# Issue order of half-height and half-width float32 products in four places of a transformer kernel

## The reference, cut to what matters

```python
# first block, sliding window attention: 8 heads of 64, 2 kv heads, window blocks of 128
s = jnp.einsum('bnqkgd,bnjkd->bnkgqj', qb, kk) * (HEAD_DIM ** -0.5)
...
o = jnp.einsum('bnkgqj,bnjkd->bnqkgd', p, vv)
# second block, first layer, latent attention: 8 heads, 128 wide without and 64 wide with rotation
s = (jnp.einsum('bqhd,bkhd->bhqk', qn, k_nope)
     + jnp.einsum('bqhr,bkr->bhqk', qr, k_rope)) * scale
# second layer, gated linear recurrence in chunks of 64 tokens, 8 heads of 128
new_state = (jnp.exp(G_last[:, :, 0, :])[..., None] * state
             + jnp.einsum('bhsd,bhse->bhde', kc * jnp.exp(G_last - G), vc))
```

## Time and profile before

| what | value |
|---|---|
| three timed runs | 3094.95, 3084.0, 3091.87 us |
| median | 3091.87 us |
| span of the profiled execution, first to last instruction | 3085.2 us |
| TensorE busy in it | 2936.1 us, 95% |
| mean granted TensorE clock | 0.984 |

### The profile page before, as it was taken

How to read it: one execution, slowest core, us unless ns; L and a number is a source line. 1 busy time by engine, 2 the same in 40 slices (tenths; PEclk the granted TensorE clock), 3 DMA queues, 4 the chain that set the end, 5 groups by cost and what they waited for, 6 DMA issues and landing times. The chain is left out here.

```text
span 3085.2 us, 42539 instructions
## 1 busy us (share of the span) xinstructions
PE 2936.1 (95%) x14433; PEld 2462.7 (80%) x14433; DVE 1818.4 (59%) x2998; ACT 1118.9 (36%) x2318; POOL 1818.0 (59%) x1154
## 2 busy tenths in 40 slices
PE   6989999999999899999999989999999999999998
PEld 5757899999999777778777667888778887788886
DVE  8764168968566488888763453222367887422226
ACT  2232225555565244444443423220135552322103
POOL 5425686676888655555534135666566674466673
PEclk9999999999999999999999999999999999999999
DMA  8422354555799999999952012233221111222331
GB/s 315 151 69 81 100 160 138 188 192 181 266 328 331 361 374 410 404 411 399 404 220 82 28 48 95 95 98 101 88 89 62 62 62 48 82 95 95 102 102 69
DMA packets 168332, 538.97 MB, mean 175 GB/s; under 512 B 16160, under 2 KB 73632, under 8 KB 151712
## 3 DMA queue, kind: packets, MB, share of 16 engines
q1 hardware_dynamic: 82544, 301.62, 28.2%
q0 software_dynamic: 18432, 134.23, 10.8%
q10 hardware_dynamic: 67248, 101.86, 9.2%
HBM read 485.21 MB, written 52.43 MB: 174 GB/s over the span
## 5 line engine op out<-in xcount | busy, mean ns | idle before, releaser
L2539 POOL TENSOR_SCALAR whi<-ring 128x1024 fp32r<-128x1024 f32 x384 | 424.1, 1104 | 969.6 <-issue 477.2
L2541 POOL TENSOR_TENSOR wlo<-ring,whi 128x1024 fp32r<-128x1024 f32 x384 | 969.8, 2526 | 32.1
L562 PE MATMUL ps<-norm_hi,whi 128*128 128x384 f32 (+1 forms) x1288 | 490.5, 381 | 15.9 <-ACT A L1414 8.8
L564 PE MATMUL ps<-norm_hi,wlo 128*128 128x384 f32 (+1 forms) x1288 | 452.4, 351 | 0.0
L563 PE MATMUL ps<-norm_lo,whi 128*128 128x384 f32 (+1 forms) x1288 | 450.4, 350 | 0.0
L562 PE MATMUL ps<-whi,mixed_hi 128*128 128x512 f32 x768 | 304.4, 396 | 25.8 <-DVE wlo L2133 23.5
L2565 POOL TENSOR_TENSOR wlo<-ring,whi 128x512 fp32r<-128x512 f32 x126 | 174.1, 1382 | 231.3 <-ACT whi L1518 231.3
L563 PE MATMUL ps<-wlo,mixed_hi 128*128 128x512 f32 x768 | 302.3, 394 | 0.0
L564 PE MATMUL ps<-whi,mixed_lo 128*128 128x512 f32 x768 | 302.2, 394 | 0.0
L562 PE MATMUL ps<-mix_hi,whi 128*128 128x512 f32 x744 | 290.7, 391 | 0.0
L564 PE MATMUL ps<-mix_hi,wlo 128*128 128x512 f32 x744 | 289.4, 389 | 0.0
(11 more groups left out here) (364 smaller groups left out, 6033.7 us busy)
## 6 DMA issues: line engine op xcount, KB each, us to landing
ring<-stream SPq DMA_DIRECT2D x519, 512.0 KB, 3.5
gelu_map<-A ACTq DMA_DIRECT2D x128, 192.0 KB, 2.9
gate_map<-A ACTq DMA_DIRECT2D x48, 512.0 KB, 5.1
A<-gelu_map ACTq DMA_DIRECT2D x128, 192.0 KB, 11.7
A<-gate_map ACTq DMA_DIRECT2D x31, 768.0 KB, 11.8
A<-ada_w SPq DMA_DIRECT2D x10, 2048.0 KB, 8.0
A<-ada_w SPq DMA_DIRECT2D x4, 1024.0 KB, 22.6
X<-x_in SPq DMA_DIRECT2D x1, 2048.0 KB, 18.6
```

The lines of the kernel that those rows point to most:

```text
L562: first = mm(out_, lh, rh, start=start, stop=False)
L564: return first, mm(out_, ll, rh, start=False, stop=stop)
L2539: g.tensor_scalar(h[:], raw[:], 1.0, 0.0, ALU.mult, ALU.add).then_inc(whi_ready, 1)
L2541: g.tensor_tensor(rest[:], raw[:], h[:].bitcast(F32), ALU.subtract).then_inc(split_ready, 1)
```

## The change

Nothing is computed differently; only the order of issue on TensorE changes. Window scores and values alternate between the halves; the latent attention issues both full products first and then the two half ones; the state changes go in the order of the chunks, so that even and odd ones alternate, and each of the last two raises `delta_ready`.

```diff
@@ win_scores(u)
-                for g in range(4):
+                for g in (0, 2, 1, 3):
                     h = kv * 4 + WIN_ORDER[g]
@@ products with the values
-                for g in range(4):
-                    h = WIN_ORDER[g]
+                for g0 in range(2):
                     for kb in kbs:
                         t0 = (n - 1 + kb) * P
-                        last = mm(ps[64 * (h % 2):64 * (h % 2) + 64, 6, (h // 2) * P:(h // 2) * P + P],
-                                  A[:, PV, t0 + kv * 64:t0 + kv * 64 + 64], ptv[:, g * 2 + kb, :],
-                                  start=kb == kbs[0], stop=kb == 1)
+                        for g in (g0, g0 + 2):
+                            h = WIN_ORDER[g]
+                            last = mm(ps[64 * (h % 2):64 * (h % 2) + 64, 6, (h // 2) * P:(h // 2) * P + P],
+                                      A[:, PV, t0 + kv * 64:t0 + kv * 64 + 64], ptv[:, g * 2 + kb, :],
+                                      start=kb == kbs[0], stop=kb == 1)
@@ mla_scores(m)
                     mm(out_, A[:, QN + h, n * P:(n + 1) * P], A[:, KN + h, 0:(n + 1) * P], start=True, stop=False)
+                for g in range(2):
+                    out_ = ps[:, 2 + g, 0:(n + 1) * P]
                     r = slice(64 * g, 64 * g + 64)
                     last = mm(out_, A[r, QR + pair, n * P:(n + 1) * P], A[r, DOWN + 4, 0:(n + 1) * P], start=False,
                               stop=True)
@@ state changes
-            def hgrn_delta(h, odd):
+            def hgrn_deltas(h):
                 if h:
                     pe.wait_ge(state_ready, (NCH - 1) * h)
-                for c in range(odd, NCH - 1, 2):
+                for c in range(NCH - 1):
+                    odd = c % 2
                     r = slice(64 * odd, 64 * odd + 64)
                     w = slice((c // 2) * P, (c // 2) * P + P)
-                    last = mm(ps[:, 3 + 2 * odd, w], A[r, HKT, w], A[r, HV + h % 2, w], start=True, stop=True)
-                last.then_inc(delta_ready, 1)
+                    ins = mm(ps[:, 3 + 2 * odd, w], A[r, HKT, w], A[r, HV + h % 2, w], start=True, stop=True)
+                    if c >= NCH - 3:
+                        ins.then_inc(delta_ready, 1)
...
-                            hgrn_delta(b, 0)
-                            hgrn_delta(b, 1)
+                            hgrn_deltas(b)
```

## The result

| kernel | runs | median, us | range, us |
|---|---|---|---|
| before | 4 | 3092.33 | 3084.0 to 3094.95 |
| changed | 4 | 3065.95 | 3064.16 to 3069.53 |

The ratio is 0.9931 with a 95% interval of 0.9918 to 0.9943: faster by 21 us (18 to 25). Forecast were 18.7 us less, 3073.2 us and a range of 3065 to 3087.

A forecast was written before the change was run, and what follows sets the result against it. TensorE, busy 95% of the span, was taken to bound the kernel. Latent scores 14.7, state changes 2.6, window values 1.4 and window scores 0 sum to 18.7 us less: 3073.2 us, range 3065 to 3087.

The forecast's parts named there:

- The five lengths said to show it: Latent scores 2.88 us (512 columns) and 0.96 (128), state changes 1.16, window values about 1.10, window scores 1.14.
- the wait of the transposes: Window attention: TensorE's wait for VectorE at the transposes of 135.39 would grow from 1.90 to about 2.4 us.
- the likeliest case: Whole kernel: the forecast itself, 18.7 us less, own range 3067 to 3079 us, chance 0.72.
- Latent scores, 14.7 us forecast: Latent attention: 2s + 0.39 us saved per unit (s one record's step), 14.8 in all, less 0.1 for staggered starts.
- the slack: Latent attention, 512 columns: probabilities ready before the transposes start; 1.3 us left after scores end 1.03 earlier.
- State changes, 2.6 us forecast: Recurrence: alternating even and odd products takes 1.09 us for 1.42, saving 0.33 in each of eight heads, all kept.
- Window values, 1.4 us forecast: Window attention: alternating saves 0.48 us in six two-block units, 2.9 in work; three units count on the path.
- Window scores, 0: Window attention: the halves already overlap when issued in two blocks, so the new order is worth 0.
- That the halves don't overlap at 512 columns: Rival, latent scores: half products gain no overlap, 6.2 us stands for 14.7, 3081.7 us in all; chance 0.08.
- the rule of the Trainium skill: Rival, latent scores: starts keep issue order, 4.3 us less gain, 14.4 in all, 3077.5 us; chance 0.04.
- rival 3: Whole kernel: waits and low clock eat most of the gain, below 9.3 us left, say 6, 3086 us; chance 0.12.
- rival 4: All changed places: each step between halves costs like a height change and overlap is lost; slower, 3124 us; chance 0.04.

The follow-up runs named there:

- window scores alone: The kernel before with the new alternating order in the window scores only; 3091.22 us.
- latent only: The kernel before with the new order in the latent scores only; median 3071.89 us, ratio 0.9949.
- the two parts alone: The kernel before with only the new latent scores, ratio 0.9949; the changed kernel with the old latent scores, ratio 0.9993.

## Why the prediction was right

**Mechanism.** Overlap of the two halves and fewer changes between full and half height, as forecast. The five lengths said to show it came out within 0.01 us: 2.87 (2.88 forecast), 0.96, 1.16, 1.09 (1.10) and 1.14. The span is 3063.2 for 3066.5. Of the other signs, the wait of the transposes and the stretches of window attention and recurrence came out otherwise (below), and one sign of being wrong appeared in one place: new idle time of 0.30 us ahead of transposes.

**The total.** The measured 3065.95 us lies 0.95 us above the lower end of the range and outside the 3067 to 3079 given for the likeliest case. The two kernels' medians differ by 26.4 us for 18.7, while the runs of the kernel before alone spread over 11 us. That the median fell inside the range is luck in part; the range's lower end had been set by that spread. The later runs gave medians of 3068.62 and 3066.64 us.

**Latent scores, 14.7 us forecast, 14.2 measured.** The units themselves save 14.8 (16 units, 1.24, 1.03, 0.82 and 0.60 by width). The missing 0.5 us is the slack. I had taken 1.3 us as the tightest case. In the third group it was less, before the change:

```profile
1744.18 2.48 DVE L2290 TENSOR_SCALAR A<-A,small 128x512 f32<-128x512 f32 x2
...
1747.36 1.09 PE L1049 MATMUL ps<-ident,A 128*128 128x128 f32 x8
```

That is 0.70 us of slack for scores that end 1.03 us earlier. After the change:

```profile
1732.89 2.47 DVE L2294 TENSOR_SCALAR A<-A,small 128x512 f32<-128x512 f32 x2
...
1735.41 0.77 PE L1052 MATMUL ps<-ident,A 128*128 128x128 f32 x5 [0.30 <-DVE A L2294]
```

The scaling of the probabilities takes 2.47 us where the earlier trace rows has 0.88, and the transposes wait for it. I had read one group and called it the tightest. Shorter scores uncovered 0.37 us of it. GpSimd computes a low part of weights (line 2545) from 1732.34 to 1734.69, just then; of the 32 scaling records only one runs beside that line, in either kernel, and it alone is long (2.07 us for 0.49). That GpSimd's work is what lengthens VectorE's is read from this one coincidence and was not tried. The other 0.12 us are in the 512-column scores of the fourth group, which in the new order start at 1752.07, right behind the end of VectorE's rotation of that pair at 1751.96 (line 2263, `rope_ready`).

**State changes, 2.6 us forecast.** Over the first seven heads the distance fell from 239.8 to 237.4 us in three profiles of the changed kernel and to 237.5 in the one without the latent part, 0.34 per head, and all of it stayed, as the waits of the earlier trace rows said; the eighth head's changes are 0.33 us shorter too. The whole stretch, 275.7 us, is only 1.6 to 1.8 shorter and not 2.6: its ends vary by themselves. From its start to the first state change it takes 7.6 us before, but 7.4 and 8.6 in two experiments that leave the recurrence as it was (window scores alone, latent only), and 8.6 in the changed kernel. One step of the working was wrong though its result held: eight pair records at 0.112 us with 0.1 for the change of height are 1.0 us and not the 0.91 of the earlier trace rows. Single starts show 0.213 us for the first step, 0.112 for the next six and 0.03 from the last record to the product with weights.

**Window values, 1.4 us forecast.** The records fell by 0.49 per unit, and where VectorE or ScalarE ends a wait the gain was returned, as said for the earlier trace rows: ahead of the head sums the waits grew from 0.36 to 0.83 and from 1.03 to 1.52 us. The wait of the transposes grew from 1.90 to 2.07 us only, where 2.4 was forecast, because 0.3 us had been given back before it:

```profile
130.00 0.70 ACT L1242 ACTIVATE A<-ps,par 128x512 f32<-128x512 f32 x1
...
130.81 0.19 PEld L562 LDWEIGHTS ps<-norm_hi,whi 128*128 128x128 f32 x1 [0.42 <-issue]
...
137.76 1.09 PE L778 MATMUL ps<-ident,A 128*128 128x128 f32 x8 [2.07 <-DVE A L1924]
```

TensorE came earlier to a product with weights whose bank ScalarE was still copying out (`bank_free`, until 130.70). From the scores to these transposes it is 16.52 us in both kernels.

Up to the products behind the normed heads (line 691), 119.5 us became 118.6, 118.0 and 117.9 in the three profiles of the changed kernel. They differ by where low clock falls: in five of the twelve profiles, old order or new, 3.4 us of it begin near 107 us and make one unit 1.6 us longer. With these compared among themselves, 119.9 (latent only, window scores alone) became 118.6; without it, 119.5 became 118.0 and 117.9. So the gain is 1.3 to 1.5 us, the forecast. Two kernels of the experiments, with another stretch of low clock at 197 us, took 119.2. The whole window stretch took 124.7 to 125.0 us in the three profiles with the old order of the values and 122.1 to 123.6 in the nine with the new one. What it gives beyond the forecast in the changed kernel, some 1 us, is clock, which was at its lower level of 1.2 GHz for longer there in the kernel before:

```profile
203.69 5.47 PE L691 MATMUL ps<-A 128*128 128x512 f32 x6 [4.23 <-DVE A L1772]
```

The changed kernel:

```profile
204.06 4.35 PE L691 MATMUL ps<-A 128*128 128x512 f32 x6 [4.23 <-DVE A L1776]
```

**Window scores, 0.** Right.

**The rivals.** That the halves don't overlap at 512 columns, and the rule of the Trainium skill (TensorE: Matmul & The Clock Gate, Part 3) that matmuls start strictly in issue order, fall. The first falls with 1.13 us for four records of 512 columns. The second falls with the order of two even and then two odd products: the other half's first record starts 0.013 us after the first of all, though four records were issued ahead of it. Where the page and these starts differ, the starts decide. What the same part says of the tiles, that they run at once, agrees with the 1.13 us. Of rival 3, the gain eaten by waits and low clock, there is only the 0.5 us in latent attention and the half of the values' 2.9 us that was forecast to go; rival 4, the slower one, falls with the window scores alone.

**The surplus.** 21.3, 20.4 and 20.7 us were measured by the ratios of three sets of runs (26.4, 18.3 and 21.1 by their medians) and 18.7 forecast; the touched places show some 18 (14.2, 2.7, and 1.3 to 1.5). About 1 us is the shorter low-clock stretch in the window; the others lie in stretches that nothing changed, vary from profile to profile, and are within the intervals. One quantity moves with them: the time at the lower clock, added up over the trace, is 99.8 us before and 86.5, 89.6 and 89.9 us in the three profiles of the changed kernel. The lower clock is half the full one, so the difference of 10 to 13 us can be worth up to 5 to 7 us where TensorE has work, an estimate and an upper bound. But it is 93.9 us in each of the two parts alone and 104.2 with the window scores alone, so it also varies by itself. Whether some of the surplus is caused by the change stays open.

## What to carry to other kernels

Cost small float32 products by their starts, in three terms: the step of a record, the price of each change between full and half height (0.19 us here), and whether two halves can run side by side. Gather half-height products so that no more than four records of one half stand ahead of the other, and the full ones apart from them. Before trusting that a gain is kept, look for the least slack in every repetition of the pattern, not in one.

## What the runs showed of the hardware

- TensorE starts products out of the order of issue when they use the other half of its rows: 0.013 us after the first with four records of the first half ahead, 0.33 with six, 0.55 with eight. With halves of the columns it is the same: 0.013 us with four ahead, 0.49 with eight (the values of the kernel before).
- Two half-height products on different rows cost what one does, also at 512 columns and when both add to banks just written: 1.13 us for four records, 1.98 when both use the same rows. The second starts 0.006 us after the first.
- Going from full to half height or back costs 0.09 us in the last record ahead of it and 0.10 us in the first behind it, at each width from 128 to 512 columns: the first step is 0.213 us for 0.112 at 128 columns and 0.533 for 0.429 at 512, and the pairs of before take eight steps and 0.68 us at all four widths (4.11, 3.26, 2.40, 1.56). A step from one half to the other costs nothing measurable.
- The same latent attention took 119.2 us at full clock and 123.4 us when one stretch of the lower clock fell on a unit of it.
